# Small experts: weight units of two experts in 8 KB runs, taken by pairs, in place of four experts in 4 KB runs

## The reference, cut to what matters

```
D_MODEL = 1024
N_EXPERTS = MOE_GROUPS * EXPERTS_PER_GROUP      # 4 * 8 = 32
TOPK_IN_GROUP = 2
EXPERT_FF = 512
...
'w_expert_gate': (DEPTH, N_EXPERTS, D_MODEL, EXPERT_FF)
'w_expert_up':   (DEPTH, N_EXPERTS, D_MODEL, EXPERT_FF)
'w_expert_down': (DEPTH, N_EXPERTS, EXPERT_FF, D_MODEL)
```

## Time and profile before

| | us |
|---|---|
| median of 3 runs | 2538.19 |
| lowest and highest run | 2534.76, 2539.86 |
| span of the profiled execution | 2526.1 |
| TensorE busy | 2151.0 (85%) |
| TensorE weight loads busy | 1617.6 (64%) |
| VectorE busy | 1426.4 (56%) |
| ScalarE busy | 1166.2 (46%) |

### The profile page before, as it was taken

One profiled execution on the slowest core, in us unless ns is written; L12 is line 12 of the kernel. 1 busy time (PEld: TensorE's weight loads), 2 busy tenths in 40 slices (PEclk: granted clock), 3 DMA queues, 4 the chain that ended last, 5 costly groups with the idle time before them and its releaser, 6 DMA issues.

```text
span 2526.1 us, 29063 instructions
## 1 busy us (share of the span) xinstructions
PE 2151.0 (85%) x11922; PEld 1617.6 (64%) x11922; DVE 1426.4 (56%) x1976; ACT 1166.2 (46%) x1521; POOL 40.9 (2%) x107
## 2 busy tenths in 40 slices
PE   6889789776655665897999888879999999999997
PEld 6867567652111111566997867668787887887875
DVE  3744535432111100434454766658889888888997
ACT  4432234320000000443443456547777787777775
POOL 0000100000000000000000000000000000000000
PEclk9989898889888888998999889789999999999999
DMA  8442651469999999476455222147989989989994
GB/s 265 167 167 84 223 178 66 171 237 409 409 409 409 409 409 404 176 289 244 146 188 183 101 100 101 67 142 275 373 319 332 379 317 366 336 317 373 331 339 190
DMA packets 267688, 656.66 MB, mean 260 GB/s; under 512 B 13454, under 2 KB 38546, under 8 KB 267544
## 3 DMA queue, kind: packets, MB, share of 16 engines
q1 hardware_dynamic: 266592, 652.90, 69.5%
q10 hardware_dynamic: 952, 1.77, 0.2%
HBM read 653.60 MB, written 1.05 MB: 259 GB/s over the span
## 4 chain that ended last, share of the span: by engine, by line
PE 68%; DMA 16%; DVE 8%; ACT 4%; issue 2%; POOL 0%; ACTq 0%; DVEq 0%; POOLq 0%
PE psum L257 17%; PE psum L258 17%; PE psum L259 17%; PE psum L252 10%; DMA ring<-in_w_expert_down 5%; DMA ring<-in_w_expert_up 5%; DMA ring<-in_w_expert_gate 5%; PE psum L2341 2%; DVE w_lo L202 2%; PE psum L880 1%; PE psum L1087 1%; ACT w_hi L192 1%; PE psum L2363 1%; DMA ring<-in_ada_w 1%; PE psum L2052 1%
## 5 line engine op out<-in xcount | busy, mean ns | idle before, releaser
L202 DVE TENSOR_TENSOR w_lo<-ring,w_hi 128x1024 fp32r<-128x1024 f32 (+1 forms) x778 | 905.0, 1179 | 391.3 <-ACT w_hi L192 378.1
L192 ACT CAST w_hi<-ring 128x1024 fp32r<-128x1024 f32 (+1 forms) x778 | 784.9, 1015 | 435.7 <-PE psum L259 430.6
L257 PE MATMUL psum<-w_hi,xg_hi 128*128 128x512 f32 (+1 forms) x768 | 293.9, 383 | 1.3 <-ACT xg_lo L2024 1.3
L259 PE MATMUL psum<-w_lo,xg_hi 128*128 128x512 f32 (+1 forms) x768 | 288.9, 376 | 0.0
L258 PE MATMUL psum<-w_hi,xg_lo 128*128 128x512 f32 (+1 forms) x768 | 288.7, 376 | 0.0
L2341 PE MATMUL psum<-ring,hT 128*32 128x512 f32 x960 | 146.6, 742 | 117.3 <-DMA ring<-in_w_expert_gate 65.6
L2341 PEld LDWEIGHTS psum<-ring,hT 128*32 128x32 f32 x960 | 29.6, 125 | 230.1 <-DMA ring<-in_w_expert_up 77.6
L257 PEld LDWEIGHTS psum<-w_hi,xg_hi 128*128 128x128 f32 x768 | 144.5, 188 | 30.5 <-issue 1.8
L258 PEld LDWEIGHTS psum<-w_hi,xg_lo 128*128 128x128 f32 x768 | 144.6, 188 | 29.2 <-issue 1.7
L259 PEld LDWEIGHTS psum<-w_lo,xg_hi 128*128 128x128 f32 x768 | 144.4, 188 | 28.6
L257 PE MATMUL psum<-w_hi,midT_hi 128*128 128x512 f32 x352 | 140.2, 398 | 3.9 <-DVE w_lo L202 3.9
(11 more groups left out here) (662 smaller groups left out, 3804.7 us busy)
## 6 DMA issues: line engine op xcount, KB each, us to landing
ring<-in_moe_w_gate SPq DMA_DIRECT2D x40, 2048.0 KB, 8.9
ring<-in_moe_w_up SPq DMA_DIRECT2D x40, 2048.0 KB, 9.5
ring<-in_moe_w_down SPq DMA_DIRECT2D x40, 2048.0 KB, 9.2
ring<-in_w_expert_gate SPq DMA_DIRECT2D x30, 2048.0 KB, 17.4
ring<-in_w_expert_up SPq DMA_DIRECT2D x30, 2048.0 KB, 17.2
ring<-in_w_expert_down SPq DMA_DIRECT2D x30, 2048.0 KB, 18.1
ring<-in_ada_w SPq DMA_DIRECT2D x24, 2048.0 KB, 8.7
ring<-in_ssm_w_in SPq DMA_DIRECT2D x10, 2048.0 KB, 7.7
```

What stands on the lines that cost most here:

```text
L192: a.copy(self.buffers(n, src.shape)[0], src).then_inc(*self.hi_made.up())
L202: v.tensor_tensor(lo, src, hi.bitcast(F32), SUB).then_inc(*self.lo_made.up())
L257: p.matmul(o, l[0], r[0], start=start, stop=False)
L259: return p.matmul(o, l[0], r[1], start=False, stop=stop)
```

## The change: what it does

The same bytes are loaded by the same number of DMAs in the same order of slots. A unit now holds half of the contraction for two of the four experts: on each partition two runs of 8 KB in place of four of 4 KB. Two units together (a pair) hold what two units held before. Since a matmul step of the group needs all four experts, TensorE now waits for both units of a pair, multiplies, and marks both as used after the last of the pair's matmuls. The number of matmuls, their shapes and the order of the sums do not change.

```diff
     def group_unit(i, g, n, w):
         if (i, g, n) in places:
-            run1.units[i, g, n] = ring.add_beside(lambda _: w[n], places[i, g, n], semaphore(f"place{g}{n}_loaded"))
+            run1.units[i, g, n] = ring.add_beside(lambda _: w[n // 2, n % 2], places[i, g, n], semaphore(f"place{g}{n}_loaded"))
         else:
-            run1.units[i, g, n] = ring.add(lambda _: w[n], UNIT)
+            run1.units[i, g, n] = ring.add(lambda _: w[n // 2, n % 2], UNIT)
...
-            w = A[name][0][GROUP * i:GROUP * (i + 1)].rearrange("e (p q k) n -> q p e (k n)", p=P, k=2)
+            w = A[name][0][GROUP * i:GROUP * (i + 1)].rearrange("(a e) (p q k) n -> q a p e (k n)", a=2, p=P, k=4)
...
-        w = A["w_expert_down"][0][GROUP * i:GROUP * (i + 1)].rearrange("e (p q) n -> q p e n", p=P)
+        w = A["w_expert_down"][0][GROUP * i:GROUP * (i + 1)].rearrange("(a e) (p q k) n -> q a p e (k n)", a=2, p=P, k=2)
...
-            for q in range(4):
-                u = run1.units[i, g, q]
-                w = ring.slot(u).rearrange("p (e k n) -> p e k n", e=GROUP, k=2)
-                p.wait_ge(*ring.loaded(u))
-                for k in range(2):
+            for q in range(2):
+                pair = [run1.units[i, g, 2 * q + n] for n in range(2)]
+                w = [ring.slot(u).rearrange("p (e k n) -> p e k n", e=2, k=4) for u in pair]
+                for u in pair:
+                    p.wait_ge(*ring.loaded(u))
+                for k in range(4):
                     for j in range(GROUP):
-                        ins = p.matmul(ps[slots_of(j), g * 512:(g + 1) * 512], M.xg[:, 2 * q + k, slots_of(j)], w[:, j, k, :],
-                                       start=2 * q + k == 0, stop=2 * q + k == KD - 1)
-                ins.then_inc(*st.pe.up("unit", u))
-                ring.empty(st.pe, u)
+                        ins = p.matmul(ps[slots_of(j), g * 512:(g + 1) * 512], M.xg[:, 4 * q + k, slots_of(j)], w[j // 2][:, j % 2, k, :],
+                                       start=4 * q + k == 0, stop=4 * q + k == KD - 1)
+                ins.then_inc(*st.pe.up("unit", pair[1]))
+                for u in pair:
+                    ring.empty(st.pe, u)
```

More of the change, by code:

```diff
@@ L2355, in group_pe @@
         ps = banks.take(p, "moe1", "down", i)
[L2356 to L2365, removed]
+        for q2 in range(2):
+            pair = [run1.units[i, 2, 2 * q2 + n] for n in range(2)]
+            w = [ring.slot(u).rearrange("p (e q n) -> p e q n", e=2, q=2) for u in pair]
+            for u in pair:
+                p.wait_ge(*ring.loaded(u))
+            for q in range(2):
+                for half in range(2):
+                    cut = slice(half * 512, (half + 1) * 512)
+                    for j in range(GROUP):
+                        ins = p.matmul(ps[slots_of(j), cut], M.midT[:, 2 * q2 + q, slots_of(j)], w[j // 2][:, j % 2, q, cut],
+                                       start=2 * q2 + q == 0, stop=2 * q2 + q == 3)
+            ins.then_inc(*st.pe.up("unit", pair[1]))
+            for u in pair:
+                ring.empty(st.pe, u)
     def group_act(a, i):
```

## The result

| | before | after |
|---|---|---|
| median, us | 2539.57 (22 runs, 2533.49 to 2546.73) | 2543.23 (22 runs, 2539.81 to 2548.15) |
| ratio | | 1.0018, 95% interval 1.0011 to 1.0026 |
| span of the profiled execution, us | 2526.1 | 2539.4 |

The changed kernel is slower by 0.18%, 4.6 us by the ratio (the medians stand 3.7 us apart), where 7.4 us less were forecast. The time lies just inside the stated range, the sign is wrong.

The account below looks back on a forecast made before the run. The prediction took moe1 to be bound by the DMA engines. Longer runs -12.5, start +1.8 and end +3.3 summed to -7.4 us, median 2538.19 to 2530.8 (chance 0.62), with a stated range of 2525 to 2543.5 us.

Parts of the forecast that it names:

- What bounds the kernel: moe1 runs at the pace of the DMA engines: 86 loads following one another at 5.12 us each.
- Longer runs, -12.5 us: moe1's loads: 8 KB packets give 421.7 GB/s, 4.973 us a unit, gaining 0.145 us on each of 86 units.
- cut runs: Rival: runs are cut at 4 KB, the rate stays 409 GB/s and only the ends remain, +5.1, 2543.3 us; chance 0.14.
- Steady state, costed at nothing: moe1 between its ends: slots freed two at a time cost nothing; tightest is the first down pair, covered by 1.6 us.
- Start, +1.8 us: First moe1 load waiting for TensorE: its slot comes free only with unit 3's, so the engines start 1.8 us later.
- End, +3.3 us: End of moe1: 32 matmuls follow the last landing, +1.7 at full clock, +5.2 at half; the middle, +3.3, taken.
- Carrying the span to the median: Whole kernel: the span goes from 2526.1 to 2518.7 us, the median from 2538.19 to 2530.8, the same -7.4.
- half gain: Rival: the longer runs in moe1 gain only half of 12.5, leaving -1.2 after the ends, 2537.0 us; chance 0.14.
- Dry engines: Rival: engines run dry at the first down pair of groups 1 to 7, 13.3 us, +5.9 in all, 2544.1; chance 0.10.
- The alternative sum of -10.6: Total if moe1's loads ran at the skill's 425 GB/s: 4.93 us a unit, a gain of 16 us.

Follow-up runs that it names:

- before_again: The kernel before, unchanged, profiled a second time; its first matmul of moe1 stood at 562.2 us and moe1 took 455.95 us.
- e2: Changed kernel's 8 KB layout, but in groups 1 to 7 TensorE takes and frees one unit at a time; 2530.59 against 2538.14 before, ratio 0.9974.
- e1: Pairs as in the changed kernel, but units in the earlier layout of four 4 KB runs; 2547.87 against 2538.14 before, ratio 1.0042.
- e4: Changed kernel plus 20 constant matmuls ahead of the waits for gate pairs and second up pairs; 2538.96 against 2537.9 before, ratio 0.9998.
- e6: 8 KB units taken one at a time, with loads issued two at a time on slots freed together; 2529.62 against 2539.6 before, ratio 0.9961.

## Why the prediction was wrong, by its own steps

*What bounds the kernel*: right. moe1 is paced by the landings in every profile.

*Longer runs, -12.5 us*: the mechanism and the pace were right. Packets are 8 KB, a load lands 4.97 us after the one ahead wherever the queue is long, and the kernels that kept it long ran at 421 GB/s. The Trainium skill ("DMA: Bandwidth & Descriptors", section SWDGE vs HWDGE vs iDMA) prefers packets of at most 4096 B, in a table on the descriptors that GpSimd builds for its DMAs. The loads here are issued by SyncE: 106.71 MB went in 13,841 packets, 13,026 of them of 8 KB, and they were faster. So the row gave no reason to expect cut runs. But from the first issue to the last landing the changed kernel took 443.2 us against 446.6: -3.4 in place of -12.5.

*Steady state, costed at nothing*: this is the step that failed. The term stood at 0 and measured about 9 us. I put the need at "about 2 us from issue to flow", the time to the first packets after an idle queue, and concluded that a pair done within 8 us of its landing was covered. What has to be covered is more: in the changed kernel loads lost time when they found less than 4.5 us, so a pair had to be done within 5.4. The pairs behind an idle wait take 5.2 to 6.2. Some 9 us of the gain went there: 12.5 us of delay, against 3.3 in the first profile of before. Nor did the engines stand idle, as the step would have it; their first packets behind such an issue were slow. The place was wrong too: the rival put the dry queue behind the first down pair. That one runs at full clock after the gather in all groups but the last, and the loads that wait for it found 4.7 us and more and lost nothing. The loads that lost were those behind the second down pair, both gate pairs and the second up pair, all of which begin after an idle wait.

*Start, +1.8 us*: right, 1.7. From moe1's first matmul to the first issue there were 5.42 us and are 7.14 (first issue at 567.63):

```profile
567.63 0.88 SPq L139 DMA_DIRECT2D ring<-in_w_expert_down  x2
```

```profile
560.49 3.64 PE L2342 MATMUL psum<-place_ns,hT 128*32 128x512 f32 x32 [1.32 <-DVE hT L2421]
```

*End, +3.3 us*: right in kind. The last pair began after 5.13 us of idle and took 5.73:

```profile
1010.94 5.73 PE L2367 MATMUL psum<-ring,midT 128*32 128x512 f32 x32 [5.13 <-DMA ring<-in_w_expert_down]
```

From the last landing to the scatter it is 7.0 us, against 3.1 in the first profile of before and 4.8 in the other three, where the last unit ran at half clock: +2.2 to +3.9. That rows 11 show it at full clock was luck.

Against before_again: +1.7 at the start, -2.6 in the stream, +2.2 at the end, 1.3 us in all, and moe1 went from 455.95 to 457.3.

*Carrying the span to the median*: the 12 us between them that I took as given were not overhead. An execution's time is 1.7 us above its span in the later runs, so the profiled execution of before was itself about 10 us faster than the median. The difference of the sums does not depend on it.

*The rivals*: cut runs and half gain are excluded by the packets and by e2. Dry engines was the right kind of rival in that the releases came too late, with the wrong place, slow packets in place of idle engines, and a price of 13.3 us where about 9 were lost. That the measured time came near that rival's 2544.1 is in part luck.

*Small slips in the sums*: 5.121 less 4.973 us, times 86, is 12.7 and not 12.5; the middle of +1.7 and +5.2 is 3.45 and not 3.3; the two cancel. The alternative sum of -10.6 comes to -10.9.

Open: why 8 KB packets need more in the queue than 4 KB ones (e1 and after differ in the layout of a unit alone). Two things in the traces bear on it; neither was tested. First, what is left counts to the landing, which is the slowest engine's. The first engine ends a load earlier, by 2.1 us at the median in the changed kernel (1.4 to 3.2) and by 1.7 in e1, so behind a landing with 4.2 us left the first engine has about 2 us, the very time from issue to flow. The loads before which it had under 2.5 us hold 11.3 of the 12.5 us of delay (26 loads; in e1 11 loads and 1.9 us, in e4 12 and 1.4). The distance of the engines by itself costs nothing: in e2, with its long queue, it is 4.4 us at the median.

Second, fetches of the program's own code share the 16 engines with the loads: the traces have 13 or 14 packets of 16 KB on the queue q8 in moe1, and 20 in e4, whose added matmuls make its program longer; each takes about 1 us. Loads that had such a fetch beside them hold 5.5 of e4's 6.2 us of delay (34 of 85 loads), 2.2 of e6's 2.3 (26), and 6.9 of the changed kernel's 12.5 (21). So with a long queue most of what is lost stands beside fetches, and e4's delay behind well-filled queues does too. A longer ring was not tried.

## What to carry to other kernels

In a stage that waits for its loads, a faster transfer is worth little if the consumer frees its buffers too late for the queue to stay full. Work out for each load what is left in the queue when it is issued, with the consumer at the slower clock that its own waiting brings about, and ask for more than the time from issue to flow: here 4.5 us were wanted where that time was 2. The traces suggest, untested, to count from the first engine that ends a load and not from the landing. Where buffers can be freed one by one, even at half the consumer's speed, as in e2, the queue stays long, TensorE stays at full clock, and most of the gain is kept. A DMA share of 1.00 does not say that nothing is lost: slow packets count as busy.

## What was not expected of the hardware

The curve of the loss against what is left in the queue: some 2 us a load under 2 us left, 1 us between 2 and 3.5, and in the changed kernel, with 8 KB packets, still 0.5 between 3.5 and 4.5, there as slow packets in engines that look busy. And TensorE's clock as part of a DMA-paced stage: the same matmuls in bursts of 32 with 4 to 7 us of idle between them had a granted clock of 0.79 over 704:964 and took 5.2 to 6.2 us where 3.64 were possible; in e2, with TensorE busy for 210 of these 260 us and 1.2 to 1.4 us of idle between units, the clock was 1.00.
